# Four of twelve modulation pieces formed in the second mixer's first blocks instead of in the first mixer

## What is computed

```
cond = jax.nn.silu(c)
mod = cond @ w_mod[l] + b_mod[l]
shift_m, scale_m, gate_m, shift_f, scale_f, gate_f = [m[:, None, :] for m in jnp.split(mod, N_MOD, axis=-1)]
h = rms_norm(x, g_mix_norm[l]) * (1.0 + scale_m) + shift_m
x = x + gate_m * hybrid_mixer(h, positions, ...)
h = rms_norm(x, g_ffn_norm[l]) * (1.0 + scale_f) + shift_f
x = x + gate_f * moe_ffn(h, ...)
```

## Time and profile before

| | us |
|---|---|
| median of 3 runs | 2139.01 |
| lowest and highest | 2130.59 and 2141.0 |
| the profiled execution | 2131.11 |
| its span in the profile | 2129.4 |

### The profile page before, as it was taken

How to read it: one execution, slowest core, us unless ns; L and a number is a source line. 1 busy time by engine, 2 the same in 40 slices (tenths; PEclk the granted TensorE clock), 3 DMA queues, 4 the chain that set the end, 5 groups by cost and what they waited for, 6 DMA issues and landing times. The chain is left out here.

```text
span 2129.4 us, 27141 instructions
## 1 busy us (share of the span) xinstructions
PE 1938.6 (91%) x8322; PEld 1324.2 (62%) x8322; DVE 1204.0 (57%) x2222; ACT 952.8 (45%) x1620; POOL 586.8 (28%) x435
## 2 busy tenths in 40 slices
PE   7989988998999997689998989989999999999992
PEld 3534434685777675367876877557766666666661
DVE  1654403536777774246164335467777777776763
ACT  2411213524656553356264323256655555555551
POOL 4799995201222222000000000022222222222211
PEclk9698989988999999799999999999999999999996
DMA  5353332263999993211202235459999999999973
GB/s 179 117 169 137 119 119 82 77 243 126 326 334 333 327 325 121 91 50 41 80 6 79 85 114 198 158 187 343 338 340 323 330 337 329 329 326 325 318 256 100
DMA packets 120531, 437.46 MB, mean 205 GB/s; under 512 B 31920, under 2 KB 36416, under 8 KB 83328
## 3 DMA queue, kind: packets, MB, share of 16 engines
q1 hardware_dynamic: 92760, 402.69, 51.1%
q0 software_dynamic: 27648, 33.67, 7.1%
q10 hardware_dynamic: 40, 0.05, 0.0%
HBM read 442.51 MB, written 63.48 MB: 238 GB/s over the span
## 5 line engine op out<-in xcount | busy, mean ns | idle before, releaser
L1620 DVE TENSOR_TENSOR big_parts<-big,h_cols_parts 128x1024 fp32r<-128x1024 f32 x384 | 460.3, 1223 | 136.7 <-ACT h_cols_parts L1673 126.0
L1673 ACT ACTIVATE h_cols_parts<-big 128x1024 fp32r<-128x1024 f32 x384 | 395.1, 1056 | 103.9 <-PE bank L1579 56.0
L1610 PE MATMUL bank<-big,heads 128*128 128x512 f32 x768 | 352.7, 602 | 1.5 <-ACT heads L1681 1.5
L1577 PE MATMUL bank<-h_cols_parts,heads_parts 128*128 128x512 f32 x768 | 310.5, 404 | 20.3 <-DVE heads_parts L1641 20.0
L1884 POOL DMA_INDIRECT acc_scratch<-heads,small x96 | 159.0, 1656 | 615.6 <-DVE small L1651 374.8
L1579 PE MATMUL bank<-h_cols_parts,heads_parts 128*128 128x512 f32 x768 | 301.7, 393 | 0.0
L1578 PE MATMUL bank<-big_parts,heads_parts 128*128 128x512 f32 x768 | 300.8, 392 | 0.0
L1610 PEld LDWEIGHTS bank<-big,heads 128*128 128x128 f32 x768 | 138.3, 190 | 139.8 <-issue 137.8
L1706 ACT ACTIVATE heads<-bank 128x512 f32<-128x512 f32 x96 | 57.4, 598 | 324.7 <-DMA acc_scratch<-heads,small 247.7
L1711 POOL MEMSET heads<- 128x2048 f32 x2 | 3.6, 1806 | 645.4 <-POOLq L1192 645.4
L1577 PEld LDWEIGHTS bank<-h_cols_parts,heads_parts 128*128 128x128 f32 x768 | 145.8, 190 | 53.0 <-DVE heads_parts L1641 13.0
(11 more groups left out here) (387 smaller groups left out, 3040.8 us busy)
## 6 DMA issues: line engine op xcount, KB each, us to landing
big<-in_w_exp_down_dram SPq DMA_DIRECT2D x96, 1024.0 KB
big<-in_w_exp_gate_dram SPq DMA_DIRECT2D x96, 1024.0 KB
big<-in_w_exp_up_dram SPq DMA_DIRECT2D x96, 1024.0 KB
big<-in_w_in_dram SPq DMA_DIRECT2D x13, 2048.0 KB, 8.8
junk<-in_w_mod_dram SPq DMA_DIRECT2D x12, 1024.0 KB, 5.1
spare<-in_w_mod_dram SPq DMA_DIRECT2D x12, 1024.0 KB, 5.2
big<-in_w_out_dram SPq DMA_DIRECT2D x4, 2048.0 KB, 10.4
h_scratch<-h_rows SPq DMA_DIRECT2D x8, 512.0 KB, 2.6
```

Of the source, the lines that this page charges most:

```text
L1577: pe.matmul(b_au[b][:, :], x_high, gu_high[:, :, c, :], start=c == 0, stop=False)
L1610: mm = pe.matmul(b_y[half][:, :], hidt[:, b, P * j:P * j + P], dn[q][:, j, 512 * half:512 * half + 512], start=j == 0, stop=j == FH - 1)
L1620: dve.tensor_tensor(gu_low[q][:, :, part, :], gu[q][:, :, part, :], gu_high[:, :, part, :].bitcast(F32), ALU.subtract).then_inc(w_low, 1)
L1673: act.activation(gu_high[:, :, part, :], gu[q][:, :, part, :], ACT.Copy).then_inc(w_high, 1)
```

## The change

Eight pieces stay in the first mixer (`FIRST_MODS`). Sums 0 to 3 stand where they stood. The sum between the `vb` rows and the `kdr` transposes goes, and so do those of iterations 0, 5 and 6; the sums behind iterations 1 to 4 are those of pieces 4 to 7. SP's queue is ordered anew around it. The other four pieces are formed by a new class, `LaterRows`: GpSimd works on their eight halves in the block of the latents (3 halves), of the latent heads (2) and in the attention over the latents (3), in the same buffers `junk` and `spare`, with accumulators in `keep` that are free there. TensorE's sums of pieces 8 and 9 stand ahead of units 0 and 8 of the attention over the latents, those of 10 and 11 at the same places of the fox attention. Both attentions have two warm-up products less. `cond` has a buffer of its own, so that it lasts.

```
             end_job(K)
-            mod_sum()
             pe.wait_ge(ops_ready, 1)
             for j in range(2):
                 turns(f"kdr{j}", [kd[:, j, P * t:P * t + P] for t in range(T)], kdr[:, :, P * j:P * j + P])
...
                               (K.q_pairs, K.k_pairs)[n][:, i, :], loop_bank())
-                if c < 7:
+                if 1 <= c <= FIRST_MODS - 4:
                     mod_sum(loop_bank())
...
                 act.activation(K.hr[part, t, 512:1024], K.bank[3][part, :], ACT.Copy).then_inc(outs_taken, 1)
-                if c < 7:
-                    copy_until(f"mod{c + 5}")
+                if 1 <= c <= FIRST_MODS - 4:
+                    copy_until(f"mod{c + 3}")
+                elif c in (3, 5):
+                    copy_until(f"pair{(c - 3) // 2}3")
...
-            act.wait_ge(mod_out, 16 * MODS)
+            act.wait_ge(mod_out, 16 * FIRST_MODS)
...
-            for k in range(2 * MODS):
+            for k in range(2 * FIRST_MODS):
...
             load_mod(4, 9)
             sp.wait_ge(K.bias_out, 16)
             sp.dma_start(K.bias_dram, bcast(K.bias_once, P)).then_inc(K.bias_spread, 16)
+            load_jobs(K, sp, 1)
             load_mod(9, 11)
             load_jobs(K, sp, 1)
-            load_mod(11, 15)
-            load_jobs(K, sp, 1)
-            load_mod(15, 18)
-            load_jobs(K, sp, 1)
-            load_mod(18, 21)
-            load_jobs(K, sp, 1)
-            load_mod(21, 2 * MODS)
+            load_mod(11, 2 * FIRST_MODS)
+            load_jobs(K, sp, 2)
             sp.wait_ge(K.bias_spread, 16)
+            sp.wait_ge(mod_used, 2 * FIRST_MODS)
             for half, place in enumerate((K.junk.rearrange("p b d -> p (b d)"), K.spare[:, :])):
-                sp.wait_ge(mod_used, 2 * MODS)
                 flat = bass.AP(K.bias_dram.tensor, P - 1 + 4 * half * BIAS_COLS, [[HEADS * BIAS_COLS - 1, P], [BIAS_COLS, 4], [1, S]])
                 sp.dma_start(place.rearrange("p (h s) -> p h s", h=4), flat).then_inc(K.bias_in, 16)
             load_jobs(K, sp, 1)
...
+FIRST_MODS = 8
...
+    sum_units = [8 * n for n in range(sums)]
...
-            for _ in range(WARM_UP):
+            for _ in range(WARM_UP - 2 if rows else WARM_UP):
                 pe.matmul(K.bank[7][:, :], K.ident[:, :], K.causal[:, :], start=True, stop=True)
             for i in range(N + 5):
+                if i in sum_units:
+                    rows.sum(pe)
...
             for i in range(N + 3):
+                if i in sum_units:
+                    rows.copy(act)
...
+            if rows:
+                rows.store(sp, 1)
+                rows.load(sp, min(halves, 2))
+                rows.store(sp, sums - 1)
         @block.gpsimd
         def _(pool):
+            if rows:
+                rows.work(pool, halves)
...
+class LaterRows:
...
+        self.K, self.w_mod = K, K.I["w_mod_2"][0]
+        self.w = [chunked(a, KC // 2, MOD) for a in (K.junk.rearrange("p b d -> p (b d)"), K.spare[:, :])]
+        self.acc = [flat[:, MOD * n:MOD * n + MOD] for n in range(4)] + [K.gain[:, MOD * n:MOD * n + MOD] for n in range(2)]
+        self.bias = K.shift[0:MODS, 0:MOD]
...
+    def load(self, sp, count):
+        for n in range(self.n_loaded, self.n_loaded + count):
+            j, half = self.half(n)
+            if n >= 2:
+                sp.wait_ge(self.used, n - 1)
+            sp.dma_start(self.w[n % 2], self.w_mod[:, MOD * j:MOD * j + MOD].rearrange("(p c) n -> p c n", p=P)
+                         [:, KC // 2 * half:KC // 2 * half + KC // 2, :]).then_inc(self.arrived[n % 2], 16)
+        self.n_loaded += count
...
+    def work(self, pool, count):
+        K = self.K
+        step = K.pool.on(pool)
+        for n in range(self.n_worked, self.n_worked + count):
+            j, half = self.half(n)
+            w, acc = self.w[n % 2], self.acc[(n // 2) % 6]
+            pool.wait_ge(self.arrived[n % 2], 16 * (n // 2 + 1))
...
+            for c in range(KC // 2):
+                cond = K.cond[:, KC // 2 * half + c:KC // 2 * half + c + 1]
+                first = half == 0 and c == 0
+                ins = pool.tensor_scalar(acc if first else w[:, c, :], w[:, c, :], cond, None, ALU.mult)
+                if not first:
+                    step(ins)
+                    ins = pool.tensor_tensor(acc, acc, w[:, c, :], ALU.add)
+                if c < KC // 2 - 1:
+                    step(ins)
+            ins.then_inc(self.used, 1)
+            pool.wait_ge(self.used, n + 1)
+        self.n_worked += count
...
+    def sum(self, pe):
+        K, n = self.K, self.n_summed
+        pe.wait_ge(self.used, 2 * n + 2)
+        pe.wait_ge(self.bias_in, 16)
+        if n:
+            pe.wait_ge(self.copied, n)
+        out = K.bank[7][0:1, :]
+        pe.matmul(out, K.ones[:, 0:1], self.acc[n % 6], start=True, stop=False)
+        j = FIRST_MODS + n
+        self.at.append(product(K, pe.matmul(out, K.ident[0:MODS, j:j + 1], self.bias, start=False, stop=True)))
+        self.n_summed += 1
...
+    def copy(self, act):
+        K, n = self.K, self.n_copied
+        act.wait_ge(K.products, self.at[n])
+        if n:
+            act.wait_ge(self.stored, 16 * n)
+        act.activation(K.mod_row[0:1, :], K.bank[7][0:1, :], ACT.Copy).then_inc(self.copied, 1)
+        self.n_copied += 1
...
+    def store(self, sp, count):
+        K = self.K
+        for n in range(self.n_stored, self.n_stored + count):
+            j = FIRST_MODS + n
+            sp.wait_ge(self.copied, n + 1)
+            sp.dma_start(K.mod_dram[MOD * j:MOD * j + MOD].unsqueeze(0), K.mod_row[0:1, :]).then_inc(self.stored, 16)
+        sp.wait_ge(self.stored, 16 * (self.n_stored + count))
+        self.n_stored += count
...
     with nc.Block(no_gpsimd_drain=True) as block:
+        @block.gpsimd
+        def _(pool):
+            K.rows2.work(pool, 3)
...
+            K.rows2.load_bias(sp)
+            K.rows2.load(sp, 4)
...
+        @block.gpsimd
+        def _(pool):
+            K.rows2.work(pool, 2)
...
         @block.sync
         def _(sp):
-            load_jobs(K, sp, 2)
+            load_jobs(K, sp, 1)
+            K.rows2.load(sp, 2)
+            load_jobs(K, sp, 1)
...
-    attention(K, "mla", 96, 0)
+    attention(K, "mla", 96, 0, rows=K.rows2, sums=2, halves=3)
...
-    attention(K, "fox", 66, 512, loads=[(K.router_w, row_blocks(K.I, "w_router_2", 0, 64), K.router_in)])
+    attention(K, "fox", 66, 512, rows=K.rows2, sums=2, loads=[(K.router_w, row_blocks(K.I, "w_router_2", 0, 64), K.router_in)])
...
```

23 lines of the change are left out of this document (20 added, 3 removed).

## The result

| | before | after |
|---|---|---|
| median | 2136.01 us (4 runs) | 2099.11 us (4 runs) |
| lowest and highest | 2130.59 and 2141.0 | 2095.56 and 2100.28 |
| profiled execution | 2131.11 | 2100.05 |
| its span | 2129.4 | 2098.2 |

The ratio is 0.9824, with a 95% interval from 0.9801 to 0.9847: faster by 1.8%. The forecast was 2109 in a range from 2097 to 2127.

What follows compares the result with a forecast made beforehand. It took TensorE to set the end of the first mixer's loop, waiting there for GpSimd. 2131.1 - 40.6 (loop) + 14.5 (second mixer) = 2105.0, raised to 2109 us for the run's level; range 2097 to 2127.

Steps and rivals of the forecast that it cites:

- The loop: First mixer's recurrent loop: its products end at 301.2 us instead of 341.8, a gain of 40.6 us.
- The split of the gain: First mixer's loop: about 15 us are waits, 12 to 13 sums removed or no longer at low clock, 13 rows at the clock.
- What is late next: First mixer's loop after the change: GpSimd's pieces are ready before their sums, none waits, with 10 us to spare.
- Rival (a): First mixer: iteration 4's weights late, or clock falls at the transposes ahead of the loop; 2112 to 2115 us, chance 0.12.
- The second mixer: Blocks that take over GpSimd's work and the sums: 2 + 6.5 + 2 + 2 + 2, a cost of 14.5 us.
- Latents: Second mixer, block of the latents: three halves on GpSimd outlast ScalarE, a cost of 2 us (1.4 to 4).
- Heads: Second mixer, block of the latent heads: two halves cost 4.4 us, plus 2 beside VectorE's rotation; 6.5 us in all.
- Transposes: Second mixer, behind the latent heads: transposes start at the low clock after TensorE stood, a cost of 2 us (0 to 4).
- Rival (c): Second mixer, attention over the latents: GpSimd's work beside it drags it by 8 us; 2117 us, chance 0.09.
- Rival (e): Second mixer: GpSimd slower there than in the first, gain eaten at factor 1.5 on a half; 2151 us at 1.8, chance 0.05.
- The 3.9 added for the run's level: Whole kernel: profiled execution lay 7.9 us under the three runs' median, so half was added, 2105.0 to 2109 us.
- Rival (b): Second mixer cheaper, 10 us instead of 14.5, rotation and cold transposes hidden; 2104 us, or 2100 at the profile's level; chance 0.10.

Runs made afterwards that it cites:

- e6: Kernel before the change, with three products on constants ahead of the wait for GpSimd at each of sums 4 to 11; 2131.59 us in one run.
- e5: Kernel before the change, with GpSimd's work on pieces 4 to 11 cut to one step in four per half, all loads and sums kept; 2096.68 us in one run.
- e7: Changed kernel with ten pieces formed in the first mixer instead of eight, four halves left for the second mixer; 2099.77 us, ratio 0.9864.
- e3: Changed kernel with GpSimd doing one step in four on each half in the second mixer, loads and sums kept; 2090.88 us.
- e12: Changed kernel with no warm-up products in the second mixer's two attentions, instead of two each; four runs: 2138.89, 2097.76, 2141.76 and 2140.36 us.

## Why the prediction was right, and where its steps were not

**The loop.** Forecast 40.6, measured 42.05. Transposes at 154.58 for 154.8; their copies and the first scores 2.3 for 2.7; iteration 0 16.0 for 16.0; iterations with sums 16.4, 16.4, 19.2, 16.4 for 16.5, 16.5, 19.3, 16.5; then 19.2, 16.4 and 15.5 for 19.3, 16.5 and 15.5. A sum 1.9. The method, rows of TensorE that don't wait, held to 1.5 us over 145.

**The reading of the bound was half wrong.** "So TensorE sets the end of this stage, and it waits there" named the wrong engine. The split of the gain into 15 of waits, 12 to 13 of sums and 13 of rows at the clock adds up, but its parts aren't causes: e6 gave the clock back and gained 0.5 at the loop's end (1.6 behind the last piece, for the 13 of the split), e5 took most of GpSimd's work away and gained 32.8 with every sum in place. The bound was seven pieces at 23.5 us up to 323, and one iteration behind it. The number came out since it was made from what is left when no sum waits, which doesn't need the split. (A piece is 15 steps, eight multiplications and seven additions, and not 16; its 22.7 us were read from the trace and are right.)

**What is late next.** "No sum waits, with 10 us to spare" was right in its outcome and thin in its margin. Piece 7 was ready at 243.2 (GpSimd's next work starts at 243.20) and not at 238 to 240, and its sum came at 246.9 and not at 250: 3.7 us. Three of GpSimd's instructions had met a VectorE instruction on 128x2048 (GpSimd's rows, then VectorE's):

```profile
196.05 3.69 POOL L844 TENSOR_SCALAR junk<-junk,cond 128x512 f32<-128x512 f32 x1
...
234.67 3.34 POOL L847 TENSOR_TENSOR h_rows<-h_rows,spare 128x512 f32<-128x512 f32 x1
238.10 3.67 POOL L844 TENSOR_SCALAR spare<-spare,cond 128x512 f32<-128x512 f32 x1
```

```profile
196.02 2.29 DVE L765 TENSOR_TENSOR big<-big,small 128x2048 f32<-128x2048 f32 x1
...
234.59 2.29 DVE L765 TENSOR_TENSOR big<-big,small 128x2048 f32<-128x2048 f32 x1
...
238.12 2.30 DVE L769 TENSOR_TENSOR big<-big,small 128x2048 f32<-128x2048 f32 x1
```

Each lost about 2.1 us, as the one at 211.41 in the earlier trace rows beside that in the earlier trace rows, and the prediction counted none, with "elsewhere POOL keeps its 1.56 and 1.26"; the trace of before has two more at 259.05 (3.60) and 262.73 (2.57). e7 ran into just these 6.3 us. By the Trainium skill ("SBUF — State Buffer", "Who interferes with whom") of a GpSimd instruction that reads SBUF and a VectorE one with two inputs there, the one that issues first keeps the other out until it is done. In the size of the loss these three rows agree, 2.1 us beside 2.29; in the order the first two do, while the third has GpSimd starting 0.02 us ahead by its record and losing all the same. Rival (a) didn't happen: the `rg` weights were issued at 216.59, as reckoned, their rows began without a gap, and the wait of 0.88 for ScalarE at 156.50 left the clock at 1.00.

**The second mixer.** Forecast 14.5, measured 15.3. Latents 2.4 for 2. Heads 5.7 for 6.5: of the 2 us for GpSimd beside the rotation 1.2 came, nearly half of them in its first instruction and not beside the rotation, and the block ended with GpSimd as said. Transposes 1.7 for 2, attention over the latents 2.9 for 2, fox attention 2.4 for 2, fox heads 0.2. e3 confirms which is whose: GpSimd's length is 8.8 of the 9.8 in the three blocks, the remaining 1.0 is within what the clock does there without any change, and the 5.3 of the attentions are sums and copies. Rival (c) is excluded by e3, too: with a quarter of GpSimd's steps that attention takes the same 53.6. Rival (e) needed a factor of 1.5 on a half; it was 1.02 (57.5 us for the five halves, 56.1 reckoned).

**The time.** The sum at the level of the profile was 2105.0, the profile says 2100.05. Of the 5.0 us 1.5 are the loop and 4.5 stretches that weren't changed, most of which is the chance of the clock in merge and router, less 0.8 in the second mixer (and 0.2 of rounding and launch). The 3.9 added for the run's level went the wrong way: the profile of before stood 4.9 under its median, that of after 0.9 above. Together 9.9. Half the miss is this term, which rested on three runs. Rival (b), 2100 to 2104, came near the time without its reason: the second mixer wasn't cheaper.

**The rest of its statements.** Four sums behind iterations 1 to 4, clock 1.00, loop end within 1.5 us: right. The blocks' ends at 872.9 and 897.3 for 877 and 902: right but for the 4.5 us that were won ahead of them (1.5 in the loop, 3.0 in the stretches behind it). The stretch from the latents to the first fox product grew by 12.7, for at most 18.

## What to carry to other kernels

Where an engine waits for another several times in a stage, look whether the other one ever stands still there. If it doesn't, it is likely the bound; take some of its work away, or fill the waits, to see. Until that pace is gone the waiting engine's clock and its number of instructions are worth next to nothing (in e6 three more products ahead of each of eight sums cost nothing, and the higher clock brought 0.5 us); cut or move the work of the pace setter, and count the stage anew from the waiting engine's undisturbed rows. Work that is moved to an idle engine of another block costs what it sticks out over the block's slowest engine: three halves in a block of 41 us and two in one of 18.6 cost 8 to 10 us of stage length that two and one did not. How much of it a launch gains has to be measured by itself: here it was 2.3 with a standard error of 2.1.

## What the runs showed of the hardware

A stage can stay at TensorE's lower clock while TensorE is busy throughout: 78 us at a granted 0.50 in the fox attention of e12, which takes 90.0 us instead of 51.0. With two 128x512 products on constants ahead of it (1.96 us) no launch did that; with none, three of four and ten of twelve did. And a stretch in which nothing is changed may move by up to 6.7 us between executions, together with its granted clock (first attention, merge and router, 150.7 in e6 to 157.4 before, with a clock of 0.93 and 0.88 in merge and router), more than most single terms of this prediction.
